# Another order of the head pairs in the two attention stages of a one-core kernel

## What is computed

```
u = modulate(rms_norm(h)); uc = modulate(rms_norm(hc))
q_w, q_g, q_n, k_*, v_* = split(u @ w_in); the same for the context (last layer: keys and values only)
y_w = window_attn(rope(q_w), rope(k_w), v_w, context keys, sink)      6 heads: banded
y_g = global_attn(rope(norm(q_g)), rope(norm(k_g)), v_g, context)     4 heads: global
y_n = neighbourhood_attn(q_n, k_n, v_n, context, rpb)                 6 heads: neighbourhood
h = h + gm * (concat(y_w, y_g, y_n) @ w_out)
```

## Time and profile before

| | us |
|---|---|
| median of 3 runs | 2401.3 (2396.16 to 2401.94) |
| the profiled execution | 2399.07 |
| its span | 2397.7 |
| PE busy | 2277.9 (95%) |
| DVE, ACT, POOL busy | 1494.5, 956.5, 367.9 |
| attention of layer 0, first scores to the last values | 447.72 to 642.43 |
| attention of layer 1, the same | 1440.88 to 1588.00 |

### The profile page before, as it was taken

How to read it: one execution, slowest core, us unless ns; L and a number is a source line. 1 busy time by engine, 2 the same in 40 slices (tenths; PEclk the granted TensorE clock), 3 DMA queues, 4 the chain that set the end, 5 groups by cost and what they waited for, 6 DMA issues and landing times. The chain is left out here.

```text
span 2397.7 us, 37075 instructions
## 1 busy us (share of the span) xinstructions
PE 2277.9 (95%) x14376; PEld 1922.0 (80%) x14376; DVE 1494.5 (62%) x2306; ACT 956.5 (40%) x1540; POOL 367.9 (15%) x365
## 2 busy tenths in 40 slices
PE   6999999998999999999999999879998999998998
PEld 4888887665678888878888876669998997798998
DVE  4666766445776666666664355566667757676774
ACT  4222223354442222242222244444446235555663
POOL 1000001000000000000000010049994675000000
PEclk8999999999999999999999999989999999999999
DMA  7554444101134444434443241114453231244444
GB/s 276 188 186 177 174 166 164 71 36 53 54 132 161 175 179 160 167 141 158 175 175 114 97 146 53 53 71 176 182 169 141 107 116 72 82 149 149 167 166 149
DMA packets 52616, 331.05 MB, mean 138 GB/s; under 512 B 6545, under 2 KB 7825, under 8 KB 21649
## 3 DMA queue, kind: packets, MB, share of 16 engines
q1 hardware_dynamic: 49040, 319.15, 36.5%
q0 software_dynamic: 3456, 10.25, 1.4%
HBM read 325.56 MB, written 3.80 MB: 137 GB/s over the span
## 5 line engine op out<-in xcount | busy, mean ns | idle before, releaser
L1173 PE MATMUL bank<-u_hi,whi 128*128 128x512 f32 (+1 forms) x2512 | 867.6, 345 | 37.9 <-DVE u_lo L1127 13.8
L1174 PE MATMUL bank<-u_lo,whi 128*128 128x512 f32 (+1 forms) x2512 | 850.8, 339 | 0.0
L1175 PE MATMUL bank<-u_hi,wlo 128*128 128x512 f32 (+1 forms) x2512 | 850.1, 338 | 0.0
L568 DVE TENSOR_TENSOR wlo<-raw,whi 128x2048 fp32r<-128x2048 f32 (+2 forms) x207 | 430.2, 2078 | 294.6 <-ACT whi L566 294.5
L1173 PEld LDWEIGHTS bank<-u_hi,whi 128*128 128x128 f32 x2512 | 478.1, 190 | 117.0 <-issue 39.0
L1175 PEld LDWEIGHTS bank<-u_hi,wlo 128*128 128x128 f32 x2512 | 478.1, 190 | 51.4
L1174 PEld LDWEIGHTS bank<-u_lo,whi 128*128 128x128 f32 x2512 | 478.5, 191 | 49.2 <-issue 0.2
L566 ACT ACTIVATE whi<-raw 128x2048 fp32r<-128x2048 f32 (+2 forms) x207 | 353.4, 1707 | 326.3 <-PE bank L1175 222.5
L1235 ACT ACTIVATE sil<-bank 128x512 f32<-128x512 f32 (+1 forms) x88 | 47.8, 544 | 543.8 <-PE bank L1175 543.8
L1173 PE MATMUL bank<-hidden_hi,whi 128*128 128x512 f32 x528 | 205.5, 389 | 0.0
L1175 PE MATMUL bank<-hidden_hi,wlo 128*128 128x512 f32 x528 | 205.5, 389 | 0.0
(11 more groups left out here) (426 smaller groups left out, 2931.0 us busy)
## 6 DMA issues: line engine op xcount, KB each, us to landing
raw<-in_stream SPq DMA_DIRECT2D x231, 1024.0 KB, 4.8
raw<-in_stream SPq DMA_DIRECT2D x80, 704.0 KB, 4.0
first_ada<-in_stream SPq DMA_DIRECT2D x8, 1024.0 KB, 16.4
raw<-in_stream SPq DMA_DIRECT2D x8, 768.0 KB, 4.4
skew<-rpb_rows POOLq DMA_DIRECT2D x8, 336.0 KB, 6.3
nbr_bias<-skew POOLq DMA_DIRECT2D x24, 112.0 KB, 3.5
h<-in_tokens SPq DMA_DIRECT2D x1, 2048.0 KB, 11.6
uq_ukv<-in_small POOLq DMA_DIRECT2D x1, 1536.0 KB, 8.1
```

Of the source, the lines that this page charges most:

```text
L568: v.tensor_tensor(self.lo[to][:, 0:n], raw[:, 0:n], self.hi[to][:, 0:n].bitcast(F32), ALU.subtract).then_inc(self.s_lo, 1)
L1173: pe.q.matmul(dst, w[0], x[0], start=start, stop=False)
L1174: pe.q.matmul(dst, w[0], x[1], start=False, stop=False)
L1175: return pe.q.matmul(dst, w[1], x[0], start=False, stop=stop)
```

## The change

The order of the pairs becomes 3, 4 (global), 0, 1 (banded), 5 (neighbourhood), 2 (banded), 6, 7 (neighbourhood). The projection tiles follow it, the rope jobs move with them, `nbr_masks` goes behind projection tile 8, and the uncharged loop before the first scores is deleted.

```
-ATT = (3, 4, 5, 6, 7, 0, 1, 2)
+ATT = (3, 4, 0, 1, 5, 2, 6, 7)
-IN_TILES = [("q", 3), ("k", 1), ("q", 4), ("v", 1), ("q", 5), ("k", 2), ("v", 2), ...
+IN_TILES = [("q", 3), ("k", 1), ("q", 4), ("v", 1), ("q", 0), ("k", 0), ("v", 0), ("q", 1), ("q", 5), ...
@@ program()
                     flush()
-                    nbr_masks()
                     yield 0
-                if i == 15:
+                if i == 6:
                     yield from turn("q", 0)
                     yield from turn("k", 0)
-            yield from v_turn(0)
-            yield from turn("q", 1)
-            yield from turn("q", 2)
+                elif i == 8:
+                    yield from turn("q", 1)
+                    nbr_masks()
+                    yield 0
+                elif i == 12:
+                    yield from turn("q", 2)
+            yield from v_turn(4)
@@ before the first scores
-        while "nbr" not in prepared:
-            next(work)
         scores(0)
```

More of the change, by code:

```diff
@@ L59 @@
 GATE_ORDER = [9, 10, 11, 0, 1, 2, 3, 4, 5, 6, 7, 8]
-ATT = (3, 4, 5, 6, 7, 0, 1, 2)
-IN_TILES = [("q", 3), ("k", 1), ("q", 4), ("v", 1), ("q", 5), ("k", 2), ("v", 2), ("q", 6), ("k", 3), ("v", 3),
-            ("q", 7), ("k", 4), ("v", 4), ("q", 0), ("k", 0), ("v", 0), ("q", 1), ("q", 2)]
+ATT = (3, 4, 0, 1, 5, 2, 6, 7)
+IN_TILES = [("q", 3), ("k", 1), ("q", 4), ("v", 1), ("q", 0), ("k", 0), ("v", 0), ("q", 1), ("q", 5), ("k", 2),
+            ("v", 2), ("q", 2), ("q", 6), ("k", 3), ("v", 3), ("q", 7), ("k", 4), ("v", 4)]
 QCHUNKS = 8
```

## The result

| | before | after |
|---|---|---|
| median of the runs, us | 2400.8 (4 runs, 2396.2 to 2401.9) | 2446.7 (4 runs, 2442.2 to 2448.4) |
| span of the profiled execution | 2397.7 | 2447.1 |

The ratio is 1.0197, with a 95% interval of 1.0183 to 1.021. The forecast was 2448 with a range of 2424 to 2474.

A forecast was written before the change was run, and what follows sets the result against it. PE, busy 95%, was taken as the bound, idle only where filler is missing. Idle 28.0 (layer 0) + 13.3 (layer 1) + clock 6 = 47.3 on 2399.1 is 2446.4; the median lies 2.2 above: 2448, range 2424 to 2474.

The forecast's parts named there:

- Layer 0, idle: PE idle in layer 0's attention: opening 9.2, six pairs 25.2, ends of runs 4.4, tail 3.0; sum 41.8 us, +28.0.
- Six pairs with ends of runs and tail: Layer 0 after the opening: six pairs at 4.2 us each (25.2), ends of forced runs 4.4, tail 3.0.
- The masks in layer 0: Masks, 3.69 us of DVE ahead of query 1's rope: 2.1 us exposed on PE, bounds 0 and 3.7.
- The masks in layer 1: Masks ahead of query 1's rope: 3.6 us exposed, as shorter tiles beside them hide less; bounds 0 and 3.7.
- Layer 1, idle: PE idle in layer 1's attention: opening 1.9, six pairs 12.3, ends of runs 6.5, tail 7.5; sum 28.2 us, +13.3.
- A pair behind a run: Layer 1: each of six pairs after a forced run of tiles idles PE 2.05 us, 12.3 in all.
- The clock: Attention of both layers: four more falls of PE's granted clock than before, +6 us, bounds 0 and +20.
- Bare stretches that cost less: Rival, chance 0.12: slots without filler lose less in pairs and opening, clock costs nothing; 2427, taken 2415 to 2430 us.
- Faster: Rival, chance 0.03: bare slots run at PE's own pace, about 3.3 us, so waits behind forced runs go; about 2394.
- A clock that stays low: Rival, chance 0.12: clock stays low through openings and behind most runs, +20 us gives 2462, with longer waits to 2480.
- Time unchanged: Rival, chance 0.03: the change does not do what it says or the account recovers; time within 0.3%.
- The signs: Profile: waits of 1.5 to 2 us before scores behind runs, bare slots of 3.7 to 4.2, mask waits 2 to 4.

The follow-up runs named there:

- the old order charged: The kernel before with only the uncharged loop before the first scores deleted, old order and masks kept: 2453.7 us, ratio 1.0219.
- the new order uncharged: The changed kernel with the uncharged loop put back, driving the generator up to key 1 before the first scores: 2389.8 us, ratio 0.9959.
- the extra matmuls: The changed kernel with unused constant matmuls in five opening slots of layer 0: eight a slot 2444.6 us, three a slot 2439.9 us.

## Why the prediction was right, and where its terms were not

The forecast of 47.3 us more (2448.6 by its sum, given as 2448), against 49.4 in the profiled executions and 45.9 between the medians, is right in mechanism and place: the debt stops `fill`, PE waits in the bare slots for the chain over ACT and DVE, and nothing behind attention gives anything back. That the charge alone does it is shown by the old order charged (+53.4) and the new order uncharged (-10.5). Term by term:

- **Layer 0, idle 41.8 forecast, 40.3 measured** to the last values. Opening 9.2 against 8.25, or 9.6 when the clock stays up. Six pairs with ends of runs and tail 32.6 against 32.1. The wait of 1.69 came back behind each run (1.87 behind the first), and the 0.68 as 0.5 to 0.8.
- **The masks in layer 0**, 2.1 forecast. The timeline of the changed kernel, DVE and PE:

```profile
516.59 3.69 DVE L1607 TENSOR_TENSOR nbr_bias<-nbr_bias,tables 128x512 f32<-128x512 f32 x6
...
518.49 0.59 PE L1589 MATMUL bank<-qT,const 128*128 128x256 f32 x2
...
520.20 0.41 DVE L1594 TENSOR_TENSOR prod<-bank,tables 128x256 f32<-128x256 f32 x1
...
521.05 0.43 DVE L1597 TENSOR_TENSOR qT<-qT,prod 128x256 f32<-128x256 f32 x1
...
521.53 0.30 PEld L1720 LDWEIGHTS bank<-kT,qT 64*128 64x128 f32 x4 [0.97 <-DVE qT L1597]
```

The rope of query 1 starts at 520.20 at the masks' end, but the scores of unit 12 wait only 0.54: the bracket of 0.97 above is that of the weight load, PE's own is 0.54, and it had six projection matmuls from 519.34 to 521.0. That cover, 1.65 us, is about the 1.4 assumed for a quarter tile. What the forecast missed is that the masks do not wait for the rope's matmul on PE (518.49): DVE started them 1.9 us ahead of it, while PE was still at the projection tile. The six pairs and the tail were larger by about 1 us without the masks, so the sum held.

- **The masks in layer 1**, 3.6 forecast. The same place, and on PE the second pair behind it:

```profile
1520.33 3.69 DVE L1607 TENSOR_TENSOR nbr_bias<-nbr_bias,tables 128x512 f32<-128x512 f32 x6
...
1525.27 2.08 PE L1720 MATMUL bank<-kT,qT 64*128 64x512 f32 x4 [3.55 <-DVE qT L1597]
...
1542.12 1.13 PE L1720 MATMUL bank<-kT,qT 64*128 64x512 f32 x4
1543.18 0.66 PE L1787 MATMUL bank<-const,probs 128*128 128x128 f32 x4
1544.62 0.63 PE L1787 MATMUL bank<-const,probs 128*128 128x128 f32 x4 [0.78 <-ACT probs_t L1794]
1545.86 1.13 PE L1720 MATMUL bank<-kT,qT 64*128 64x512 f32 x4 [0.62 <-ACT probs L1757]
1547.38 0.66 PE L1787 MATMUL bank<-const,probs 128*128 128x128 f32 x4 [0.39 <-ACT probs_t L1794]
```

3.55 before the scores of unit 6; and taking the masks away there gave 3.8 (opening uncharged). Here the masks start only behind two weight splits of DVE, 0.9 us after the rope's matmul (1519.45), and the cover is again six projection matmuls, which end at 1521.7.

- **Layer 1, idle 28.2 forecast, 21.3 measured.** This is the step that was mis-sized. A pair behind a run was to cost 2.05 and 0.4 for its end; five pairs measured 7.96 without the masks' wait, 1.6 each. The rows show the waits of one: 0.78 (the copy), 0.62 (the exponentials) and 0.39 (the copy). The window from which 2.05 was read the earlier trace rows held another wait, which the timeline of PE before shows:

```profile
1549.42 0.66 PE L1784 MATMUL bank<-const,probs 128*128 128x128 f32 x4 [1.74 <-DVE probs L1770]
```

1.74 for normalised exponentials on a DVE that was busy 7.39 of 8.42 there. That wait belongs to single pairs and not to each: of the five it shows in one of the changed kernel, as 1.14 (before the transposes at 1565.99), and with the masks back at the head it is there at 1.73 in the pair that had the wait for the masks. Why these pairs have it was not tested. A mean of a window was carried over to six pairs without its causes. The last pair and the tail were to cost 2.45 and 7.5; they cost 6.57 together; which of their parts was missing was not taken apart. The opening was larger than forecast, 3.22 against 1.9 and 0.5 for the end of its run.

- **The clock, +6 forecast.** PE's busy time in both stages grew by 14.8, above the +6 and inside the bounds of 0 and +20. The number of falls was nearly right: in windows of 4 us the clock is below 1.00 in seven places from first scores to last values, against four before, where four more were forecast. Their length was not. The +6 took some 1.5 for each, from one window of 4 us (whose mean of 0.57, between levels of 0.50 and 1.00, means 3.4 of 4 us at the lower one, not half of PE's work); but the opening stays low for 20 us, and two other places, 528 to 540 and 1524 to 1536, are below 1.00 for three windows each. In elapsed time the share is smaller, since part of it filled waits: 3 to 4 us in the opening of layer 0, shown by the extra matmuls. For layer 1 two executions of the same kernel differ: 150.45 busy in 176.62 here, 146.79 in 173.02 when it ran again, so 3.6 us there come and go with PE's busy time, without an edit. For the other pairs of layer 0 the share was not measured apart.
- **What cancelled.** Idle was forecast 41.3 above before and came to 34.0, 7.3 less; the clock was 8.8 more than forecast. (The 41.3 goes by windows to the last values, the 34.0 by windows to the norm; to the last values it came to 33.0.) With both errors the total still came within 2.1 us of the measured one; that it came so near is luck. That closeness says less of the working than the figure suggests: layer 0's idle term was good, layer 1's a third too large, and the clock's less than half of what it was.
- **The rivals.** Bare stretches that cost less: true of layer 1 alone, by some 7 us. Faster: PE idles in every one of the windows above. Scores-to-scores times of 3.3 to 3.4 us do occur in layer 0 (543.88 to 547.29, 606.06 to 609.37), shorter than the loop of 3.74, but with waits of PE in them. A clock that stays low: in layer 0 the opening has 0.80, and of the six windows behind it three have 1.00 and three 0.85 to 0.94; in layer 1 the opening has 0.87, one pair 0.71, one 0.99 and the last 0.94, and three have 1.00. So it stays low through one opening and one pair, not behind most runs. Time unchanged: the account never recovered, as the old order charged shows too.
- **The signs.** The waits of 1.5 to 2 before scores came behind every run of layer 0 (1.69 to 1.87), but are 0.16 to 0.80 in layer 1. Scores-to-scores times of 3.7 to 4.2 in bare token slots: 3.7 to 3.9 in layer 1 where the clock is full, 3.4 to 3.6 and 4.1 to 4.4 in layer 0. The wait of 2 to 4 for the rope behind the masks came in layer 1 (3.55) and not in layer 0 (0.54).

## What to carry to other kernels

Where an account decides how much independent work is put between the links of a dependent chain, ask of every edit what it charges. Work that must be done before the loop starts is a fixed cost; booked as a debt it starves the loop for a whole stage (57 us here, for 32 and 24 us of booked cost), and each later forced step renews the debt. Carry a window's idle time over to another place only after its waits have been read one by one, and test a change of order and a change of accounting apart: together they were 46 us slower, the order with an uncharged start and the masks kept at the head 16.5 us faster.

## What the runs showed of the hardware

In the opening of layer 0 the granted clock was down in all eleven profiles: 0.50 to 0.67 from 448 to 452, or 0.62 from 452 to 456 in the one that had 1.00 before. With projection matmuls between the slots (the kernel before) PE was busy 4.00 of 4 us and the clock was at 1.00 from 456 on, and in the kernels with an uncharged opening and no debt it was 0.98 to 1.00 from 452 to 456. In the bare opening of the changed kernel's first profile it was at 0.50 from 456 to 468, though PE was busy 2.1 to 4.0 of every 4, and scores took 2.08 in place of 1.13 us. Fifteen matmuls of 128 columns, 4.6 us of work in all, kept it at 0.96 to 1.00 from 452 to 468 and made the stage 3 to 4 us shorter: work that is thrown away can pay where PE waits in short pieces. Forty of them kept the clock as well and left the opening at 42.9 us. The copy behind the first set of transposes ended PE's wait of 0.78 in six of the seven bare places of layer 1 in the changed kernel, at the low clock (1529.17) as at the full one; in the seventh it was the normalised exponentials (1.14).
